# A hybrid decoder step on one Trainium2 core: 24 of the 64 operand copies of the value compression are dropped, and TensorE reads those operands with a step

## What is computed

```python
def compress_blocks(kv_cmp, cmp_pos_emb, w_cmp_k, w_cmp_v, k_norm_cmp_g):
    # kv_cmp: (b, tokens, 2, 2 heads, 64); blocks of 64 tokens
    blk = pad_to_blocks(kv_cmp) + cmp_pos_emb[None, None, :, None, None, :]
    kc = jnp.einsum('bnlkd,lde->bnke', blk[:, :, :, 0], w_cmp_k)   # w_cmp_k, w_cmp_v: (64, 64, 64)
    vc = jnp.einsum('bnlkd,lde->bnke', blk[:, :, :, 1], w_cmp_v)
    return rmsnorm(kc, k_norm_cmp_g), vc
```

## Time and profile before

| | before |
|---|---|
| device time, median of 3 runs | 719.79 us (716.7 to 721.31) |
| profiled execution: span from its first to its last instruction | 718.1 us |
| mean granted clock of TensorE | 0.985 |
| TensorE matmul busy | 677.8 us, 94% |
| VectorE, ScalarE, GpSimd busy | 282.9, 169.9, 276.2 us |
| HBM traffic | 192.50 MB, 268 GB/s |

### The profile page before, as it was taken

One profiled execution on the slowest core, in us unless ns is written; L12 is line 12 of the kernel. 1 busy time (PEld: TensorE's weight loads), 2 busy tenths in 40 slices (PEclk: granted clock), 3 DMA queues, 4 the chain that ended last, 5 costly groups with the idle time before them and its releaser, 6 DMA issues.

```text
span 718.1 us, 14980 instructions
## 1 busy us (share of the span) xinstructions
PE 677.8 (94%) x5708; PEld 339.7 (47%) x5708; DVE 282.9 (39%) x746; ACT 169.9 (24%) x359; POOL 276.2 (38%) x429
## 2 busy tenths in 40 slices
PE   6999999999969989998999998999999999999993
PEld 3555455875656655876555554333333333333320
DVE  1210026128779877877112156214102500520036
ACT  3200021137645673644022120001000100010100
POOL 2466246888477574874000003404400610200050
PEclk9999999999989999999999998999999999999997
DMA  8967605047940399999892076999999999999965
GB/s 287 278 171 246 182 29 117 10 135 216 247 123 4 114 303 319 303 280 279 288 430 104 31 277 199 354 412 387 421 405 419 421 418 408 420 424 410 399 243 212
DMA packets 90207, 192.50 MB, mean 268 GB/s; under 512 B 17018, under 2 KB 60442, under 8 KB 83854
## 3 DMA queue, kind: packets, MB, share of 16 engines
q1 hardware_dynamic: 72133, 150.10, 58.7%
q0 software_dynamic: 13136, 33.30, 14.2%
q10 hardware_dynamic: 4864, 8.13, 3.0%
HBM read 174.63 MB, written 17.25 MB: 267 GB/s over the span
## 4 chain that ended last, share of the span: by engine, by line
PE 56%; DVE 5%; DMA 2%; issue 1%; ACT 1%; DVEq 0%; SPq 0%; ACTq 0%
PE bank L1482 34%; PE bank L1376 8%; PE bank L1318 2%; DVE xh L2458 2%; DMA xh<-in_state_win_kv 1%; PE bank L1396 1%; PE bank L1520 1%; PE bank L1367 1%; PE bank L1166 1%; PE bank L1221 1%; PE bank L1254 1%; DMA proj<-normed_rows,idx 1%; PE bank L1224 1%; PE bank L1213 1%; PE bank L1196 1%
## 5 line engine op out<-in xcount | busy, mean ns | idle before, releaser
L1482 PE MATMUL bank<-arena,proj 128*32 128x512 f32 x1728 | 237.8, 596 | 0.8 <-issue 0.8
L1482 PEld LDWEIGHTS bank<-arena,proj 128*32 128x32 f32 x1728 | 66.9, 110 | 120.8 <-issue 119.9
L996 PE MATMUL bank<-arena,amT 128*128 128x454 f32 x256 | 101.9, 556 | 0.8 <-DVE amT L1878 0.8
L2712 POOL DMA_INDIRECT proj<-normed_rows,idx_of_quads x40 | 45.0, 1125 | 141.1 <-DVE proj L2417 125.8
L2603 POOL DMA_DIRECT2D arena<-in_cache_cmp_kv x128 | 68.6, 536 | 52.2 <-issue 44.5
L996 PEld LDWEIGHTS bank<-arena,amT 128*128 128x128 f32 x256 | 48.9, 194 | 49.7 <-issue 48.5
L1482 PE MATMUL bank<-amT,proj 128*32 128x512 f32 x288 | 70.1, 592 | 0.0
L2610 POOL DMA_DIRECT2D arena<-in_cache_slc_kv x96 | 56.8, 594 | 16.4 <-PE bank L1013 5.8
L2426 DVE TENSOR_TENSOR proj<-proj,bank 128x512 f32<-128x512 f32 x12 | 8.3, 688 | 138.0 <-PE bank L1482 138.0
L2623 POOL COPY arena<-arena 128x268 f32<-128x268 f32 x64 | 37.9, 655 | 26.4 <-PE bank L993 19.0
L1482 PE MATMUL bank<-queries_and_bias,proj 128*32 128x512 f32 x288 | 42.7, 593 | 0.0
(11 more groups left out here) (417 smaller groups left out, 1011.3 us busy)
## 6 DMA issues: line engine op xcount, KB each, us to landing
arena<-in_w_down SPq DMA_DIRECT2D x24, 1024.0 KB, 17.3
arena<-in_w_up SPq DMA_DIRECT2D x10, 2048.0 KB, 18.1
arena<-in_w_gate SPq DMA_DIRECT2D x16, 1024.0 KB, 15.1
arena<-in_cache_cmp_kv POOLq DMA_DIRECT2D x128, 64.0 KB, 2.5
arena<-in_cache_cmp_kv SPq DMA_DIRECT2D x128, 64.0 KB, 2.2
arena<-in_w_gate SPq DMA_DIRECT2D x4, 2048.0 KB, 20.2
amT<-in_w_gate SPq DMA_DIRECT2D x6, 1024.0 KB, 17.7
arena<-in_w_in SPq DMA_DIRECT2D x3, 1816.0 KB, 10.0
```

The costliest lines, as they stand in the source:

```text
L996: last = pe.matmul(ps(("in", c, i))[0:n, 0:WC], xnT[:, k, i * P:i * P + n], w_in[c % 2][:, k, :], start=k == 0, stop=k == KC - 1)
L1482: ins = pe.matmul(dst[part, :], rows[:, part], own if q < TRIO else shared, start=start, stop=stop)
L2712: po.indirect_dma_start(xg[j % 2][:, q * QD:(q + 1) * QD], None, scratch["n2"].rearrange("n (a c) -> (n a) c", a=QUADS), bass.IndirectOffs ...
```

## The change

Of the value compression's odd steps, those with d < `COPIED` = 48 (24 steps: 1, 3, ... 47) are no longer copied. Their moving operand is `chunk_in(d)` itself, 134 floats with a step of 64 floats, read from the pages. The even steps and the odd ones from 49 on are copied as before; `nth_copy` counts only copied steps in the ring, so 13 chunks now span up to 26 steps. TensorE waits at step 1 for the prompt's blocks (which GpSimd puts into the cache before its first copy). SyncE's first load over the pages waits for fewer copies of VectorE and ScalarE, and also for TensorE's step 47.

```diff
+COPIED = 48
...
         def chunk_out(r, d):
 
-            return chunks[r][d % RING].rearrange("p g (n h) -> p g n h", h=KVH)
+            return chunks[r][nth_copy(r, d) % RING].rearrange("p g (n h) -> p g n h", h=KVH)
+
+        def nth_copy(r, d):
+
+            if r == 0:
+                return d
+            return d // 2 if d < COPIED else COPIED // 2 + d - COPIED
+
+        def copied(r, d):
+
+            return r == 0 or d % 2 == 0 or d >= COPIED
 
         def chunk_free(eng, r, d):
 
-            n = r * (HD - 1) + d - RING
-            if d < RING:
+            n = nth_copy(r, d) - RING
+            if n < 0:
                 if r:
                     for par in range(2):
                         filled(eng, ("cmp", 0, par))
             else:
-                eng.wait_ge(chunk_used, n + 1)
+                of = n if r == 0 else 2 * n if n < COPIED // 2 else n - COPIED // 2 + COPIED
+                eng.wait_ge(chunk_used, r * (HD - 1) + of + 1)
...
             sp.wait_ge(regrouped, regrouped_at(1, HD - 2))
-            sp.wait_ge(by_vector, HD // 4)
-            sp.wait_ge(by_scalar, HD // 4)
+            sp.wait_ge(by_vector, (HD - COPIED) // 4)
+            sp.wait_ge(by_scalar, (HD - COPIED) // 4)
+            sp.wait_ge(chunk_used, HD - 1 + COPIED)
             load_slc(0, 0, 2)
...
                 if by_pool(r, d):
                     pe.wait_ge(regrouped, regrouped_at(r, d))
-                else:
-                    pe.wait_ge((by_vector, by_scalar)[d % 4 // 2], d // 4 + 1)
+                elif copied(r, d):
+                    pe.wait_ge((by_vector, by_scalar)[d % 4 // 2], (d - COPIED) // 4 + 1)
+                elif d == 1:
+                    pe.wait_ge(regrouped, regrouped_at(0, HD - 1) + 1)
                 for par in range(2):
                     rows = slice(64 * par, 64 * par + 64)
                     for g in range(2):
+                        part = chunks[r][nth_copy(r, d) % RING][rows, g, :] if copied(r, d) else chunk_in(d)[rows, g, :, :]
                         last = pe.matmul(ps(("cmp", r, par))[64 * g:64 * g + 64, 0:2 * SIDE], w_cmp[r][rows, d, :],
-                                         chunks[r][d % RING][rows, g, :], start=d == 0, stop=d == HD - 1)
+                                         part, start=d == 0, stop=d == HD - 1)
...
-                    if r == 1 and d % 4 == 3:
+                    if r == 1 and d % 4 == 3 and d >= COPIED:
                         sc.wait_ge(regrouped, regrouped_at(0, HD - 1) + 1)
                         chunk_free(sc, r, d)
                         sc.activation(chunk_out(r, d), chunk_in(d), ACT.Copy).then_inc(by_scalar, 1)
...
-                    if r == 1 and d % 4 == 1:
+                    if r == 1 and d % 4 == 1 and d >= COPIED:
                         ve.wait_ge(regrouped, regrouped_at(0, HD - 1) + 1)
                         chunk_free(ve, r, d)
                         ve.tensor_copy(chunk_out(r, d), chunk_in(d)).then_inc(by_vector, 1)
```

## The result

The changed kernel took 724.55 us (median of 11 runs, 722.09 to 730.95), the kernel before 720.37 us beside it (11 runs, 716.70 to 723.07). The ratio over all executions is 1.0078, with a 95% interval of 1.0058 to 1.0097: 5.6 us slower (4.2 to 7.0; the two medians alone lie 4.2 us apart). I had forecast 719.7 us, no difference. The time lies inside the range given, but the kernel moved, and the price of a strided step was taken over four times too small: 0.085 us where 0.37 was measured.

A forecast was written before the change was run, and what follows sets the result against it. TensorE was taken as the bound, VectorE nearly beside it. Gains of 1.5 us against a strided-read price of 1.36 us gave -0.1 us, so 719.7 us against a median of 719.79; range 715.8 to 728 us.

The forecast's parts named there:

- The bound: Mixed stretch of prompt attention and value compression: TensorE sets the pace, busy 30.14 of 32 us, VectorE nearly beside it.
- The relief: Twelve VectorE and twelve ScalarE copies removed; counts only where TensorE waits: 1.20 + 0.29 = 1.5 us gained.
- The wait before step 9: Second step of unit 13, TensorE waiting for a late VectorE copy: the gap goes, gain 1.20 us.
- The first copy: Start of the stretch: GpSimd's first copy falls from 952 ns to the 660 median, gain 0.29 us.
- The wait before step 49: Second step of unit 18, still copied: TensorE's wait for VectorE's copy stays at 0.55 us, gain 0.
- The price of the strided read: Direct steps on TensorE: 0.085 us more each; twenty cost 1.7 us, 1.36 us after 0.34 us is swallowed.
- nearest row: Strided stationary loads in gathered-row transposes, one float in eight: 0.21 ns more a read, 0.64 ns, so 343 ns a step.
- the second wait: TensorE's 0.55 us gap before step 49 in unit 18; swallows unit 17's 0.34 us of strided price.
- The four steps of unit 12: At granted clock 0.50 a step takes 0.44 us, so a 343 ns strided read hides there at no cost.
- The rival of the doubled read: Direct steps: every strided read takes twice its time, +4.1 us, 723.9 us; chance 0.19.
- The rival of the other side: Direct steps: TensorE reads as badly as ScalarE, 0.53 us more a step, +10.7 us, 730.5 us; chance 0.13.
- GpSimd's lead: GpSimd's ring of 13 spans 26 steps, so it runs further ahead; nothing hangs on it, no cost.

The follow-up runs named there:

- relief_alone: Changed kernel, direct steps reading 134 adjacent floats (wrong values), crowded-expert branch never taken; 717.16 us beside 718.68 for the kernel before, ratio 0.9977.
- relief_short_lead: As relief_alone, but GpSimd's copy for step d waits for step d-13 as before the change; 717.17 us beside 718.79, ratio 0.9977.
- step_1: Changed kernel, direct steps reading 134 adjacent floats (wrong values, crowding the experts); read only up to 250 us: eight units 18.0 us against 20.05 before.
- weights_strided: Kernel before, stationary weights of 24 odd steps read one float in 64, moving operand contiguous (wrong values); executed once, 719.36 us, unit 13 2.25 us.
- change_short_lead: Changed kernel with right values, GpSimd's copy for step d waiting for step d-13 as before the change; 726.08 us, ratio 1.0083.

## Why the prediction was wrong

**The bound** was read rightly. TensorE sets the pace of the stretch: what its steps cost more went through to the end, 5.65 us in the eight units and 5.6 in the runs.

**The relief** was right in sum, as closely as the runs can tell, and partly by luck. I had 1.5 us; relief_alone and relief_short_lead measured 1.5 and 1.6. The wait before step 9 gave 1.4 us where I had 1.20. The first copy gave 0.20 where I had 0.29, from a misread row. Left out of the sum were 0.5 us of small waits in units 14 and 15, which have no gap of their own in a merged timeline; starts give them. The wait before step 49, which I said would stay, stayed in one trace with no strided price (0.60 us) and shrank to 0.3 us in two others (relief_alone, step_1). In the changed kernel it was swallowed, as said.

**The price of the strided read** is the step that failed, and in it the "nearest row". I took 0.64 ns a read from the strided transposes, by charging the 0.027 us between their pitch and the contiguous one to 128 reads. That takes the load and the stream of a transpose to lie one after the other. weights_strided shows that they lie mostly beside each other. The whole pitch of 0.136 us can then belong to the 128 loads, 1.06 ns a read. The trace of before had a sign of it in the records of the loads themselves, strided and contiguous:

```profile
L1467 PEld LDWEIGHTS bank<-mats,proj x16: 185/202/226, 439.6 to 447.0; 128*128 128x128 f32 x16
...
L1221 PEld LDWEIGHTS bank<-mats,arena x64: 137/140/143, 273.6 to 323.2; 128*128 128x128 f32 x64
```

The eight strided loads at full clock, from 446.22, take 193 ns in the median, 53 more than the contiguous 140, while the pitch is only 27 longer. By the records a read costs 0.43 + 53 / 128 = 0.84 ns. So the row gave 0.84 to 1.06 ns, and the term would have been 20 x (536 x 0.84 ns - 258 ns), less the 0.55 us that the second wait swallows, 3.3 us, and 5.7 us in the same way from 1.06 ns, not 1.36. That 1.06 ns gives just the duration measured, 0.57 us a step, is luck, as the moving operand takes 0.86 ns at the distance of that row (one in eight) and 1.06 only at one in 64.

Measured it is 0.37 us for each of 20 steps and 4.32 - 3.46 = 0.86 us in unit 12, together 8.3 us, against which stand 2.7 us of waits gone or swallowed. The forecast had named 0.25 us a step as the point from which it is wrong, and 2.4 us for a mixed unit; the units took 3.48.

The four steps of unit 12, which I had hidden behind the half clock, are not hidden: a direct step takes 0.57 to 0.58 us at either clock and a copied one 0.44 at the half. That is 0.14 us for each of the four, 0.6 of the 0.86 us. The rest fits TensorE's earlier start: it went through all of unit 12 at half clock, while before the clock was back up from 215 us on (0.94).

**The rival of the doubled read** had the mechanism and nearly the size (+4.1 us). Its condition, "every strided read takes twice its time", is what one in four to one in 63 show; one in 64 takes 2.5 times. The rival of the other side, ScalarE's price, named 0.53 us more a step; 0.37 was measured, just under the 0.39 from where the kernel would be over 1% slower.

**GpSimd's lead** was put at nothing. That holds in time: change_short_lead is no faster than the changed kernel. But I looked only at who waits for GpSimd, not at whom it holds up. VectorE's mask operations take longer beside its copies, and the 3.55 us of relief_alone show what such a meeting can cost, once in these traces.

## What to carry to other kernels

Dropping a copy by reading with a step moves its cost from the engine that copied to the one that reads. Here the copies lay almost wholly under TensorE's work, where they cost some 1.5 us, and the strided read lay on it. Before such a step, count the reads per partition over all matmuls that share it, and look whether two neighbouring reads still fall into 16 bytes. A price taken from the difference of two pitches holds only if what is differenced doesn't overlap; bound it once as if everything overlapped, too.

## What the runs showed of the hardware that I had not expected

- For a moving operand read with a step it counts whether neighbouring reads share 16 bytes, and hardly how far apart they are: 0.23 us a step of eight records at one float in one, 0.24 in two, 0.46 in four, 0.44 to 0.47 in eight to 63. One in 64, the changed kernel, takes 0.57; why is open.
- That time does not follow TensorE's clock: 0.57 us at the full one and 0.58 at the half, where the contiguous step goes from 0.23 to 0.45.
- VectorE operations with two inputs take longer beside GpSimd's copies: the ten mask operations 5.81 us when GpSimd copies all the while, 4.64 when it stops after seven of them. Once, one such operation took 3.55 us instead of 0.42, until just behind the end of GpSimd's run. The Trainium skill says of the pair ("SBUF — State Buffer", "Who interferes with whom") that the shared ports are an exclusive lock and that a VectorE instruction with two such inputs contends with GpSimd's reads; the traces agree, and the 3.55 us are longer than any single instruction of GpSimd's in that run.
